# Norm statistics as four columns per tile, and modulation weights as the stationary operand, in a two-block transformer kernel

## What is computed

```
def rmsnorm(x, g):
    return x * rsqrt(mean(x * x, axis=-1) + 1e-6) * g
def modulate(h, shift, scale):
    return h * (1.0 + scale) + shift

# block 1; c and c_ctx are vectors of 1024, w_ada is 1024 x 6144
sh1, sc1, gt1, sh2, sc2, gt2 = split(silu(c) @ w_ada + b_ada, 6)
csh1, csc1 = the first two of split(silu(c_ctx) @ w_ada + b_ada, 6)
hc = modulate(rmsnorm(ctx, g_pre_mix), csh1, csc1)
hx = modulate(rmsnorm(x, g_pre_mix), sh1, sc1)
yx = token_mixers(hx @ w_in, states from hc, ...)     # gated linear attention, 4 heads of 128, and a short convolution
#    inside: rmsnorm(o, g_head) over the 128 values of each head
x = x + gt1 * rmsnorm(yx @ w_out, g_post_mix)
hx = modulate(rmsnorm(x, g_pre_ffn), sh2, sc2)
x = x + gt2 * rmsnorm(conv_ffn(hx), g_post_ffn)
# block 2
h = rmsnorm(x, attn_norm);  x = x + (gated pooling and windowed attention of h) @ w_out
h = rmsnorm(x, ffn_norm);   x = x + ffn(h)
```

## Time and profile before

| | us |
|---|---|
| three timed runs | 1599.45, 1601.71, 1605.25 |
| median | 1601.71 |
| span of the profiled execution, first to last instruction | 1596.6 |
| PE busy in it | 1475.8 (92%) |
| DVE busy | 783.6 (49%) |
| ACT busy | 398.1 (25%) |
| POOL busy | 816.1 (51%) |
| mean granted TensorE clock (1 is full speed) | 0.954 |

### The profile page before, as it was taken

How to read it: one execution, slowest core, us unless ns; L and a number is a source line. 1 busy time by engine, 2 the same in 40 slices (tenths; PEclk the granted TensorE clock), 3 DMA queues, 4 the chain that set the end, 5 groups by cost and what they waited for, 6 DMA issues and landing times.

```text
span 1596.6 us, 19471 instructions
## 1 busy us (share of the span) xinstructions
PE 1475.8 (92%) x6832; PEld 1153.6 (72%) x6832; DVE 783.6 (49%) x1152; ACT 398.1 (25%) x726; POOL 816.1 (51%) x651
## 2 busy tenths in 40 slices
PE   6999889999699999999988986999898999999998
PEld 3567668777378888878846865788685888887887
DVE  5469778775666666620025097333615444453001
ACT  2340223331232222210022202254403333232001
POOL 0234234324466666666655674433265666666664
PEclk9989989989899999999988998999899999999999
DMA  9447311111123333322221321211121333332321
GB/s 314 140 158 257 99 44 50 54 40 53 53 66 93 92 92 92 93 92 92 92 66 40 94 78 53 80 53 40 40 81 51 93 95 100 94 92 79 105 92 66
DMA packets 184291, 141.98 MB, mean 89 GB/s; under 512 B 5515, under 2 KB 164784, under 8 KB 184240
## 3 DMA queue, kind: packets, MB, share of 16 engines
q1 hardware_dynamic: 182373, 140.11, 29.1%
q10 hardware_dynamic: 1867, 1.18, 0.2%
HBM read 139.17 MB, written 2.10 MB: 88 GB/s over the span
## 4 chain that ended last, share of the span: by engine, by line
PE 75%; DVE 16%; issue 3%; ACT 3%; POOL 1%; DMA 1%; SPq 0%; POOLq 0%; DVEq 0%; ACTq 0%
PE ps L478 22%; PE ps L480 21%; PE ps L479 21%; PE ps L545 2%; DVE ada_acc L1527 2%; PE ps L715 2%; PE ps L518 1%; PE ps L966 1%; DVE norm_rinv L1467 1%; DVE g_z L1628 1%; PE ps L936 1%; PE ps L952 1%; DVE pw L1896 1%; DVE SS L1709 1%; DVE c_p L1686 1%
## 5 line engine op out<-in xcount | busy, mean ns | idle before, releaser
L433 POOL TENSOR_TENSOR w_lo<-raw,w_hi 128x1024 fp32r<-128x1024 f32 x209 | 508.1, 2431 | 17.4
L478 PE MATMUL ps<-h_hi,w_hi 128*128 128x512 f32 x1064 | 437.3, 411 | 43.1 <-DVE h_lo L1481 16.9
L480 PE MATMUL ps<-h_hi,w_lo 128*128 128x512 f32 x1064 | 427.9, 402 | 0.0
L479 PE MATMUL ps<-h_lo,w_hi 128*128 128x512 f32 x1064 | 426.4, 401 | 0.0
L429 POOL TENSOR_TENSOR w_hi<-raw,cst 128x16 fp32r<-128x16 f32 x209 | 58.2, 279 | 687.5 <-PE ps L480 620.6
L478 PEld LDWEIGHTS ps<-h_hi,w_hi 128*128 128x128 f32 x1064 | 204.6, 192 | 100.5 <-issue 38.3
L480 PEld LDWEIGHTS ps<-h_hi,w_lo 128*128 128x128 f32 x1064 | 204.3, 192 | 50.7
L479 PEld LDWEIGHTS ps<-h_lo,w_hi 128*128 128x128 f32 x1064 | 205.1, 193 | 46.4
L430 POOL TENSOR_SCALAR w_hi<-raw 128x1008 fp32r<-128x1008 f32 x209 | 224.6, 1075 | 0.0
L1791 DVE SCALAR_TENSOR_TENSOR f_acc<-ps,par,f_acc 128x441 f32<-128x441 f32 (+2 forms) x176 | 122.3, 695 | 56.7 <-ACT f_acc L1030 34.4
L478 PE MATMUL ps<-f_hi,w_hi 128*128 (+1 forms) x352 | 140.5, 399 | 5.2 <-POOL w_lo L433 5.2
(11 more groups left out here) (268 smaller groups left out, 1949.4 us busy)
## 6 DMA issues: line engine op xcount, KB each, us to landing
raw<-in_w_up SPq DMA_DIRECT2D x88, 512.0 KB, 3.8
raw<-in_w_in SPq DMA_DIRECT2D x59, 512.0 KB, 3.9
raw<-in_w_down SPq DMA_DIRECT2D x44, 512.0 KB, 3.5
v_tok<-in_w_ada SPq DMA_DIRECT2D x18, 512.0 KB, 5.9
ada_first<-in_w_ada SPq DMA_DIRECT2D x8, 1024.0 KB, 12.5
raw<-in_w_out SPq DMA_DIRECT2D x16, 512.0 KB, 3.6
ada<-in_w_ada SPq DMA_DIRECT2D x14, 512.0 KB, 5.0
x_tok<-in_x SPq DMA_DIRECT2D x2, 1024.0 KB, 8.6
```

Of the source, the lines that this page charges most:

```text
L433: pool.tensor_tensor(w_lo[:, slot % 2, :], raw[:, slot, :], w_hi[:, slot % 2, :].bitcast(F32), ALU.subtract).then_inc(S("lo_split"), 1)
L478: nc.tensor.matmul(dst, lhs_hi, rhs_hi, start=first, stop=False)
L479: nc.tensor.matmul(dst, lhs_hi, rhs_lo, start=False, stop=False)
L480: return nc.tensor.matmul(dst, lhs_lo, rhs_hi, start=False, stop=last)
```

## The change

- The constants `ones` of 128 columns become one column `mean` (1/1024), and `head_mean` (4/128) for the heads.
- Sums: `sum_squares` and `sum_tiles` take 128 x 128 blocks of the squares as stationary operand and the one column `mean` as moving one: four matmuls (two for the context) give a tile of 128 tokens by four columns. ACT's root and DVE's reciprocal work on 128 x 4.
- A new step `spread`: PE multiplies each column, broadcast to 128 x 128 as stationary operand, by the identity (four matmuls of 128 columns), so that bank 7 (6 for k=1) holds the reciprocal on all partitions. `scaled` reads it from PSUM; for k=2 and 4 ACT copies it to `norm_rinv` first, since the bank is needed at once by the next `sum_tiles`.
- The heads in the same way, with `head_spread`; `head_root` (now `head_roots`) and the reciprocal move from level 3 and 4 to level 2, the scaling to level 3. `diagonal` and output tile 7 now wait for `head_scaled`, where they waited for the root. Two waits for `head_scaled` on DVE and ACT go, since `c_p` is no longer used for the reciprocal.
- The modulation pairs take w_ada as stationary operand in blocks of 128 x 128 and the condition (128 x 2) as the moving one: sixteen matmuls a pair. The result is in columns, so the copies and L582 go, and SP and DVE wait for the last pair instead of `ada_turned`.
- In the opening ACT squares three tiles of x before the condition's Silu, and does the rest of the norms before its small DMA issues. `sum_squares` stands after pair 3 and 5 (before: 1 and 3), the spreads after pair 4 and 6.
- Waits of PE for `norm_rooted` before it overwrites the bank become waits for `norm_scaled`.

```diff
+    token_root, token_rinv = sb("token_root", [P, 7, 4]), sb("token_rinv", [P, 7, 4])
+    head_root, head_rinv = sb("head_root", [P, CHUNKS, GH]), sb("head_rinv", [P, CHUNKS, GH])
+    def stat_bank(k):
+        return 6 if k == 1 else 7
@@ SP
                     if u0 + i == 3:
-                        sp.wait_ge(S("ada_turned"), 1)
+                        sp.wait_ge(S("ada_first_used"), ADA_PAIRS)
@@ PE
         def ada_pair(n):
             pe.wait_ge(ada_first_loaded[n % FIRST_SLOTS], 16 * (n // FIRST_SLOTS + 1))
-            for t in range(KT):
-                mm = nc.tensor.matmul(ps[0:2, 2 + n // 2, (n % 2) * 256:(n % 2) * 256 + 256], cond[:, t, :],
-                                      ada_first[:, n % FIRST_SLOTS, t, :], start=(t == 0), stop=(t == KT - 1))
+            for m in (2 * n, 2 * n + 1):
+                for t in range(KT):
+                    mm = nc.tensor.matmul(ps[:, 5, 2 * m:2 * m + 2], ada_first[:, n % FIRST_SLOTS, t, (m % 2) * P:(m % 2 + 1) * P],
+                                          cond[:, t, :], start=(t == 0), stop=(t == KT - 1))
             mm.then_inc(S("ada_first_used"), 1)
         def sum_squares(k, n):
             pe.wait_ge(S("norm_added"), 7 * k + 7)
-            if k >= 1:
-                pe.wait_ge(S("norm_rooted"), k)
-            nc.tensor.matmul(ps[:, 7, 0:n], const("ones", P), norm_acc[:, 0:n], start=True, stop=True).then_inc(S("norm_ss"), 1)
+            for t in range(n // P):
+                mm = nc.tensor.matmul(ps[:, stat_bank(k), t:t + 1], norm_acc[:, t * P:(t + 1) * P], const("mean"),
+                                      start=True, stop=True)
+            mm.then_inc(S("norm_ss"), 1)
+        def spread(k, n, done):
+            pe.wait_ge(S("norm_inverted"), k + 1)
+            for t in range(n // P):
+                mm = nc.tensor.matmul(ps[:, stat_bank(k), t * P:(t + 1) * P], token_rinv[:, k, t:t + 1].broadcast_to([P, P]),
+                                      const("ident", P), start=True, stop=True)
+            mm.then_inc(S(done), 1)
         def sum_tiles(k, bank_free):
-            pe.wait_ge(S("norm_rooted"), k)
+            pe.wait_ge(*bank_free)
             for m in range(KT):
                 pe.wait_ge(S("norm_squared"), KT * k + m + 1)
-                nc.tensor.matmul(ps[:, 7, :], const("ones", P), norm_sq[:, m % 2, :], start=(m == 0), stop=(m == KT - 1))\
-                    .then_inc(S("norm_ss" if m == KT - 1 else "square_used"), 1)
+                for t in range(BLOCKS):
+                    mm = nc.tensor.matmul(ps[:, 7, t:t + 1], norm_sq[:, m % 2, t * P:(t + 1) * P], const("mean"),
+                                          start=(m == 0 and t == 0), stop=(m == KT - 1), skip_group_check=True)
+                mm.then_inc(S("norm_ss" if m == KT - 1 else "square_used"), 1)
         for n in range(ADA_PAIRS):
             ada_pair(n)
-            if n == 1:
+            if n == 3:
                 sum_squares(0, T)
-            elif n == 3:
+            elif n == 4:
+                spread(0, T, "rinv_ready")
+            elif n == 5:
                 sum_squares(1, TC)
-        for m in range(16):
-            if m % 4 == 0:
-                pe.wait_ge(S("ada_rows"), m // 4 + 1)
-            mm = nc.tensor.matmul(ps[:, 6, 2 * m:2 * m + 2], v_tok[0:2, m // 4, (m % 4) * P:(m % 4 + 1) * P],
-                                  cst[0:2, CONST["ident"]:CONST["ident"] + 2], start=True, stop=True)
-        mm.then_inc(S("ada_turned"), 1)
+            elif n == 6:
+                spread(1, TC, "rinv_ready")
...
             if c >= 1:
-                pe.wait_ge(S("o_rooted"), c)
+                pe.wait_ge(S("head_scaled"), c)
         def head_sums(c):
             pe.wait_ge(S("o_squared"), c + 1)
-            nc.tensor.matmul(ps[:, 6, :], const("ones", P), c_sc[:, :], start=True, stop=True).then_inc(S("o_ss"), 1)
+            for h in range(GH):
+                mm = nc.tensor.matmul(ps[:, 6, h:h + 1], c_sc[:, h * P:(h + 1) * P], const("head_mean"), start=True, stop=True)
+            mm.then_inc(S("o_ss"), 1)
+        def head_spread(c):
+            pe.wait_ge(S("o_inverted"), c + 1)
+            for h in range(GH):
+                mm = nc.tensor.matmul(ps[:, 6, h * P:(h + 1) * P], head_rinv[:, c, h:h + 1].broadcast_to([P, P]),
+                                      const("ident", P), start=True, stop=True)
+            mm.then_inc(S("o_spread"), 1)
...
                 if n == 1 and c >= 1:
                     head_sums(c - 1)
+                if n == 2 and c >= 1:
+                    head_spread(c - 1)
...
         out_tile("out_s", 6, ys_hi, ys_lo, 0)
-        pe.wait_ge(S("o_rooted"), CHUNKS)
+        head_spread(CHUNKS - 1)
+        pe.wait_ge(S("head_scaled"), CHUNKS)
         out_tile("out_s", 7, ys_hi, ys_lo, 0)
...
         sum_squares(2, T)
-        sum_tiles(3, None)
+        spread(2, T, "rinv_spread")
+        sum_tiles(3, (S("rinv_ready"), 3))
+        spread(3, T, "rinv_ready")
...
         sum_tiles(4, (S("mo_copied"), 2))
-        sum_tiles(5, None)
+        spread(4, T, "rinv_spread")
+        sum_tiles(5, (S("rinv_ready"), 5))
+        spread(5, T, "rinv_ready")
...
         sum_tiles(6, x_done(2, 0))
+        spread(6, T, "rinv_ready")
@@ ACT
-            activate(norm_root[:, 0:n], ps[:, 7, 0:n], ACT.Sqrt, bias=const("eps"), scale=1.0 / D).then_inc(S("norm_rooted"), 1)
+            activate(token_root[:, k, 0:n // P], ps[:, stat_bank(k), 0:n // P], ACT.Sqrt, bias=const("eps")).then_inc(S("norm_rooted"), 1)
...
-            act.wait_ge(S("rinv_ready"), k)
             root(k)
+            act.wait_ge(S("rinv_spread"), k // 2)
+            activate(norm_rinv[:, :], ps[:, 7, :], ACT.Copy).then_inc(S("rinv_ready"), 1)
@@ DVE
-            vec.reciprocal(rinv[:, 0:n], norm_root[:, 0:n]).then_inc(S("rinv_ready"), 1)
+            vec.reciprocal(token_rinv[:, k, 0:n // P], token_root[:, k, 0:n // P]).then_inc(S("norm_inverted"), 1)
...
+        def head_invert(c):
+            dve.wait_ge(S("o_rooted"), c + 1)
+            vec.reciprocal(head_rinv[:, c, :], head_root[:, c, :]).then_inc(S("o_inverted"), 1)
         def head_scale(c):
-            dve.wait_ge(S("o_rooted"), c + 1)
-            order.done(vec.reciprocal(c_p[:, :], c_p[:, :]))
-            order.wait()
+            dve.wait_ge(S("o_spread"), c + 1)
```

More of the change, by code:

```diff
@@ L56 @@
 CONST_COLS = 0
-for _name, _n in [("ident", P), ("upto", P), ("from", P), ("ones", P), ("band", 2 * P), ("sign", 1), ("nsign", 1),
-                  ("eps", 1), ("eps4", 1), ("one", 1), ("zero", 1), ("half_pi", 1), ("inv_freq", HALF_ROPE),
+for _name, _n in [("ident", P), ("upto", P), ("from", P), ("ones", 16), ("mean", 1), ("head_mean", 1),
+                  ("band", 2 * P), ("sign", 1), ("nsign", 1), ("eps", 1), ("eps4", 1), ("one", 1), ("zero", 1), ("half_pi", 1), ("inv_freq", HALF_ROPE),
                   ("inv_count", 16 * len(POOL_WINDOWS))]:
@@ L71, in shape_constants @@
     put("from", (i[:, None] >= i[None, :]) * 1.0)
-    put("ones", np.ones((P, P)))
+    put("ones", np.ones((P, 16)))
+    put("mean", np.full((P, 1), 1.0 / D))
+    put("head_mean", np.full((P, 1), 4.0 / DV))
     k = np.arange(2 * P)
@@ L629, in _ @@
         pe.wait_ge(S("mod_ready"), 1)
-        pe.wait_ge(S("norm_rooted"), 2)
+        pe.wait_ge(S("norm_scaled"), 2 * KT)
         for u in (3, 4):
@@ L857, in _ @@
         token_units("q2a", 2, 512, 0, True)
-        pe.wait_ge(S("norm_rooted"), 6)
+        pe.wait_ge(S("norm_scaled"), 4 * KT)
         token_units("q2b", 2, 512, 4, False)
@@ L1070, in shifted @@
                 activate(normed(m), normed(m), ACT.Identity, bias=shift(m)).then_inc(S("shifted"), 1)
+        x_square = lambda m: square(0, m, lambda m: xT[:, m, :], lambda m: act.wait_ge(S("turned_out"), m + 1))
+        for m in range(3):
+            x_square(m)
         act.wait_ge(S("turned_out"), 10)
@@ L1075, in _ @@
         activate(cond[:, :, 1], column("c_ctx", 0, KT), ACT.Silu).then_inc(S("cond_ready"), 1)
+        for m in range(3, KT):
+            x_square(m)
+        for m in range(KT):
+            square(1, m, lambda m: ctxT[:, m, :], lambda m: act.wait_ge(S("turned_out"), 10 + m // 2 + 1), TC)
+            if m == 2:
+                root(0)
+        root(1, TC)
         act.wait_ge(S("gw_cleared"), 2)
@@ L1086, in _ @@
             act.dma_start(positions[:, :], a["positions_2"].rearrange("(t p) -> p t", p=P)).then_inc(S("heads_loaded"), 16)
[L1087 to L1096, removed]
         act.wait_ge(S("mod_ready"), 1)
@@ L1217, in head_square, with head_roots @@
                 .then_inc(S("o_squared"), 1)
-        def head_root(c):
+        def head_roots(c):
             act.wait_ge(S("o_ss"), c + 1)
-            act.wait_ge(S("branch_dve"), 3 * min(c + 1, CHUNKS - 1) + 3)
-            if c == CHUNKS - 1:
-                act.wait_ge(S("head_scaled"), c)
-            activate(c_p[:, :], ps[:, 6, :], ACT.Sqrt, bias=const("eps4"), scale=4.0 / DV).then_inc(S("o_rooted"), 1)
```

(29 more changed lines are left out.)

24 lines of the change are left out of this document (10 added, 14 removed).

## The result

The changed kernel takes 1618.93 us (median of 4 runs, 1618.03 to 1620.53); the kernel before, in the same comparison, 1601.91 us (4 runs, 1599.45 to 1605.25). The ratio is 1.0098, 95% interval 1.0085 to 1.0112: slower by 1%. The profiled execution spans 1616.0 us against 1596.6.

A forecast was written before the change was run, and what follows sets the result against it. PE bounds the kernel (75% of the chain), standing still at stage joints. Terms 22.6 - 3.9 + 0.4 + 3.6 + 1.1 = +23.8 take the span from 1596.6 to 1620.4; plus 5.1 gives 1625.5 us, range 1605 to 1634.

The forecast's parts named there:

- The clock: In the opening's new pairs: they start at half clock and never raise it, 0.50 throughout.
- rival 1: Throughout the kernel: small passes hold and raise the clock as any others, so 1581, faster; chance 0.13.
- 4 (1588): Heads' loop: extra passes and DVE's waits eat the heads' gain at high clock, about -14, 1588; chance 0.04 with Rival 3.
- The price of a small pass: For each small PE record: 0.107 us at full clock and 0.213 at half, bounds 0.107 and 0.24.
- Rival 3: In the pairs: a load takes the same time at either clock, about -23, 1579; chance 0.04 with 4 (1588).
- The opening: Modulation pairs, first sums and spreads: 256 pair records at half clock end the stage later, +22.6 us, bounds +19 to +30.
- The heads: Heads' loop and behind its last chunk: spreads cost +3.4, shorter waits and clock losses gain more; sum -3.9, bounds -8 to +1.
- k=2 and k=3: Joint after the mixer: k=2 gains 1.85, k=3's tiles at half clock cost 3.8, its tail gains 1.5; +0.4.
- k=4 and k=5: Block 1's end: sums cost +2.6 and +3.4, tails give -0.9 and -1.5; +3.6.
- k=6: Sums of 7.60 us grow by 2.6 and the tail gives 1.5: +1.1.
- Rival 2: Opening pays, but at the sum tiles the squares' pace and lucky clock turns hide the cost: +6.0, 1608; chance 0.09.

The follow-up runs named there:

- pairs_only: The kernel before with only the new modulation pairs (w_ada stationary, copies and L582 gone), norms as before: 1624.36 us, ratio 1.0146.
- pairs_wide: The changed kernel with the condition in the pairs broadcast from two to 128 streamed columns: 1600.66 us, ratio 0.9984.
- pairs_undone: The changed kernel with the old modulation pairs, copies and L582 back, norms and heads as changed: 1601.20 us, ratio 0.9995.
- all_wide: pairs_wide with every small sum, of tokens and heads, also streaming 128 columns: 1581.60 us, ratio 0.9887.
- sums_wide: The changed kernel with only its sums, of tokens and heads, widened to 128 columns, pairs kept narrow: 1603.67 us, ratio 1.0004.
- after_again: The changed kernel once more, unedited, for comparison on one chip: 1619.68 us, ratio 1.0106.
- wide_early: all_wide with the opening's sum 0 after pair 1 instead of 3 and its spread after pair 3 instead of 4: 1574.84 us, again 1576.52 us.

## Why the prediction was right, point by point

**The clock.** I took it that passes with two streamed columns don't raise the clock, on the strength of L582. They don't: 0.50 from 20.64 to 80.5 us with PE busy throughout, and in `pairs_only` it fell to 0.50 under them. `pairs_wide` shows that it is the streamed columns (and the output that goes with them), since nothing else of the pairs was changed. Rivals 1 (1581) and 4 (1588), which need a high clock, fall by the same windows. Part 1 of the Trainium skill's page "TensorE: Matmul & The Clock Gate" lets sustained work release the gate; by the profile's busy column this case disagrees, 4.00 of 4.00 at 0.50 for 60 us.

**The price of a small pass.** 0.213 us at half clock: 6.83 for 32 is 0.213. At full clock `pairs_wide` has 3.74 for 32, 0.117, within the rows I had (0.107 taken). Rival 3 (a load costs the same at either clock) falls: in `pairs_only` the load of one and the same instruction took 192 ns at 1.00 and 333 ns at 0.50. The estimate of 0.107 us from the Trainium skill ("TensorE: Matmul & The Clock Gate", LDWEIGHTS), which names no clock, doesn't hold in a stretch at half clock, where a record takes 0.213. One row was misread: the 64 records from 40.96 are four pairs and not eight; their 0.218 us each is right.

**The opening.** Forecast +22.6 from the pairs' start; measured +22.8, less 1.1 because the pairs began earlier (20.64 for 21.74). Since `pairs_undone` is at 0.9995, this is also the cause of the loss. One statement beside the sum was wrong: that the cover of ACT and DVE would be enough at full clock too. With fast pairs PE waited 3.84 us (`pairs_undone`) and 3.90 us (`pairs_wide`) for DVE's adds. Here the slow pairs hid it, so it cost the forecast nothing; rival 1's gain of 3.8 us in the opening was too good by it (`all_wide`, with a high clock, has `mod` at 59.38, 0.6 later than before).

**The heads.** Forecast −3.9, measured −4.4. In the loop I had put spreads (+3.4) against lost waits and a lost fall of the clock (−3.35); net it was +0.3. The pauses of 0.75 and 0.70 and the fall near 283.5 are indeed gone; the spreads' price was not measured by itself. Behind the last chunk −4.7 for my −4: the wait ahead of output tile 7 is 0.84 (forecast 0.8), the one for the low parts that I had allowed 0.9 for did not come, and `out_g` runs at full clock, as forecast.

**k=2 and k=3.** 3.48 us from the sum to the first product, forecast 3.5; sum tiles 13.79, forecast 13.7. The joint: +0.45, forecast +0.4.

**k=4 and k=5.** Forecast +3.6, measured +4.9: the term that was mis-sized is k=4's sums. I let the clock hold for 3.4 us and took +2.6; they grew by 3.9 (11.38 for 7.50). The tail of k=4 (−0.9) and all of k=5 (+3.45 and −1.5) came as forecast. The windows of k=4, after:

```profile
834.00:835.00 1.00, 1.00 (x11) 1.00 (x11) 0.00 (x0) 0.41 (x2) 0.92 (x2) 1.00 0.14 53
835.00:836.00 1.00, 0.87 (x8) 0.79 (x7) 0.00 (x0) 0.98 (x2) 1.00 (x1) 0.85 0.03 8
836.00:837.00 1.00, 1.00 (x6) 1.00 (x7) 0.00 (x0) 0.04 (x1) 0.56 (x1) 0.50 0.00 0
```

The change of pace midway is there, after 3 us. **k=6**, where it held until 1221.4, grew by 2.0 for my 2.6: +0.5, forecast +1.1. The single +2.6 taken for both was 1.3 too little for k=4 and 0.6 too much for k=6. Rival 2 (the sum tiles' cost is hidden) falls with the 1.71 us a tile, and `sums_wide` shows 16 us to be had there.

**What I had not counted.** The first mixer gave 1.0 and block 2's attention 1.6 with no change in their work: in q2a the clock rose 4.2 us behind the first pass, before 5.8. The first of these is within what one kernel does between two profiles (`after_again` gave it +0.9); the second came again in `after_again`. And I added 5.1 from span to median, as before; after, the difference was 2.9. In every execution on record for which both are known, the time lies 1.7 to 3.3 us above its own span, so the span of 1596.6 belongs to the shortest of the three runs (1599.45), and 2.3 of the 5.1 were that run's distance from the median. Change: forecast +23.8, measured +17.0 by the medians. Span: forecast 1620.4, measured 1616.0, of which 2.6 are those two stages and 1.1 the early start; time: 1625.5 against 1618.93.

**What stays open.** Why stages with unchanged work differ by a few microseconds between kernels: from `mod` to the first level it was 147.5 to 151.4 us over twelve profiles. The clock's edges fall in other places in them; what sets an edge was not isolated.

## What to carry to other kernels

Count streamed columns, not instructions: products that only needed one or two columns, behind loads of 128, held TensorE at 1.2 GHz here while it looked fully busy, and reading the same operand with a broadcast to 128 columns made it faster, in the pairs and in the sums alike. Make statistics narrow on VectorE, where a reciprocal of 128 x 512 costs 3.35 us and one of 128 x 4 costs 0.18, and keep them wide on TensorE. When a stage is made faster, look again at what its length was covering: here sum 0's later place cost nothing behind slow pairs and 5 us behind fast ones.

## What the runs showed of the hardware

One record of a single-precision product (a product is two) of 128 x 128 by two columns takes 0.213 us at half clock, and one by 128 columns 0.117 at full clock: 64 times the columns in little more than half the time. The load scales with the clock too (median 333 ns in the changed kernel's pairs, 191 in `pairs_wide`, and 192 then 333 within `pairs_only`). Eight sums with one streamed column span 0.95 us at full clock and eight with 128 span 1.05. The clock can also differ between two profiles of one kernel over the same instructions, as the two lines of `wide_early` above show, and the 17 runs of the kernel before in one comparison scatter over 12 us (1595.50 to 1607.38).
